# Entering RWKV time mixing by halves of tokens and features, with half of the split subtractions on POOL

## The reference

```python
h = rms_norm(x, g_mix[layer])
x = x + rwkv7_time_mix(h, ...)
...
h_prev = jnp.pad(h, ((0, 0), (1, 0), (0, 0)))[:, :-1]
hh = h_prev - h
xr = h + hh * mu[0]
xw = h + hh * mu[1]
xk = h + hh * mu[2]
xv = h + hh * mu[3]
xa = h + hh * mu[4]
xg = h + hh * mu[5]
r = xr @ w_r
w = -jax.nn.softplus(-(w0 + jnp.tanh(xw @ w1) @ w2)) - 0.5
k = xk @ w_k
v = xv @ w_v
a = jax.nn.sigmoid(a0 + (xa @ a1) @ a2)
g = jax.nn.sigmoid(xg @ g1) @ g2
```

## Time and profile before

| what | us |
|---|---|
| three runs: median (lowest to highest) | 1528.77 (1528.56 to 1530.85) |
| the profiled execution: its own time | 1527.23 |
| its span in the profile | 1525.4 |
| PE busy in the span | 1419.9 |
| DVE busy | 921.0 |
| ACT busy | 723.3 |
| POOL busy | 156.4 |

### The profile page before, as it was taken

How to read it: one execution, slowest core, us unless ns; L and a number is a source line. 1 busy time by engine, 2 the same in 40 slices (tenths; PEclk the granted TensorE clock), 3 DMA queues, 4 the chain that set the end, 5 groups by cost and what they waited for, 6 DMA issues and landing times.

```text
span 1525.4 us, 25988 instructions
## 1 busy us (share of the span) xinstructions
PE 1419.9 (93%) x10678; PEld 1214.7 (80%) x10678; DVE 921.0 (60%) x1250; ACT 723.3 (47%) x974; POOL 156.4 (10%) x132
## 2 busy tenths in 40 slices
PE   8998999998999999979988987999999968799998
PEld 8966988887988899867767765799997745589997
DVE  5565655566566645569868687465455655455563
ACT  5464545446545545445644342454445645254452
POOL 0162011100000111010120111000000232000000
PEclk9999999999999999989989999999999989799999
DMA  8733565555545655644442000556464531246562
GB/s 294 240 93 111 188 191 186 183 165 189 191 152 165 214 173 175 209 150 131 145 146 84 4 4 18 161 177 208 152 226 152 166 96 42 83 151 195 159 210 88
DMA packets 82262, 231.32 MB, mean 152 GB/s; under 512 B 11696, under 2 KB 17472, under 8 KB 82144
## 3 DMA queue, kind: packets, MB, share of 16 engines
q1 hardware_dynamic: 81584, 227.54, 46.6%
q0 software_dynamic: 560, 2.11, 0.4%
HBM read 228.56 MB, written 1.06 MB: 151 GB/s over the span
## 4 chain that ended last, share of the span: by engine, by line
PE 77%; DVE 8%; issue 5%; ACT 4%; POOL 3%; DMA 1%; DVEq 0%; ACTq 0%; POOLq 0%; SPq 0%
PE PS L410 48%; PE PS L413 26%; PE PS L425 4%; ACT SH L382 1%; POOL SM L539 1%; DVE XI L1264 1%; POOL AB L770 1%; DVE SL L385 1%; DVE SL L388 1%; DVE AB L744 1%; POOL QK L1895 0%; POOL SM L836 0%; ACT JK L542 0%; ACT AB L754 0%; DVE LG L1552 0%
## 5 line engine op out<-in xcount | busy, mean ns | idle before, releaser
L388 DVE SCALAR_TENSOR_TENSOR SL<-ST,SM,SH 128x1024 fp32r<-128x1024 f32 (+1 forms) x256 | 314.8, 1249 | 171.8 <-ACT SH L382 121.7
L382 ACT ACTIVATE SH<-ST,SM 128x1024 fp32r<-128x1024 f32 (+1 forms) x256 | 282.2, 1121 | 219.7 <-PE PS L413 133.1
L410 PE MATMUL PS<-XH,SH 128*128 128x256 f32 x1256 | 353.3, 281 | 2.6 <-DVE XL L1269 1.3
L413 PE MATMUL PS<-XH,SL 128*128 128x256 f32 x1256 | 353.4, 281 | 0.0
L410 PE MATMUL PS<-XL,SH 128*128 128x256 f32 x1256 | 352.4, 281 | 0.0
L385 DVE TENSOR_TENSOR SL<-ST,SH 128x1024 fp32r<-128x1024 f32 (+1 forms) x167 | 215.8, 1308 | 155.4 <-ACT SH L382 137.9
L410 PE MATMUL PS<-SH,XH 128*128 128x512 f32 x576 | 240.0, 417 | 26.6 <-DVE XL L1753 8.3
L382 ACT ACTIVATE SH<-ST 128x1024 fp32r<-128x1024 f32 (+1 forms) x167 | 172.1, 1047 | 177.6 <-PE PS L413 151.8
L410 PEld LDWEIGHTS PS<-XH,SH 128*128 128x128 f32 x1256 | 237.3, 189 | 4.2 <-ACT SH L382 3.0
L410 PEld LDWEIGHTS PS<-XL,SH 128*128 128x128 f32 x1256 | 235.1, 187 | 0.9
L413 PEld LDWEIGHTS PS<-XH,SL 128*128 128x128 f32 x1256 | 235.2, 187 | 0.2
(11 more groups left out here) (312 smaller groups left out, 1450.7 us busy)
## 6 DMA issues: line engine op xcount, KB each, us to landing
ST<-in_ffn_w_gu SPq DMA_DIRECT2D x80, 512.0 KB, 4.7
ST<-in_w_mlp_up SPq DMA_DIRECT2D x64, 512.0 KB, 4.8
ST<-in_w_mlp_down SPq DMA_DIRECT2D x64, 512.0 KB, 4.4
ST<-in_ffn_w_down SPq DMA_DIRECT2D x44, 512.0 KB, 4.3
ST<-in_w_attn_in SPq DMA_DIRECT2D x24, 512.0 KB, 5.2
ST<-in_w_conv_in SPq DMA_DIRECT2D x24, 512.0 KB, 4.5
ST<-in_w_ple_gate SPq DMA_DIRECT2D x16, 512.0 KB, 4.2
ST<-in_kv_w SPq DMA_DIRECT2D x16, 512.0 KB, 4.2
```

What stands on the lines that cost most here:

```text
L382: a = ac.do(lambda e: e.activation(h[p0:p1, 0:cols], t[p0:p1, 0:cols], ACT.Copy, scale=sc), ready, t_gt, pe_done.get(i - NSPLIT))
L388: b = ve.do(lambda e: e.scalar_tensor_tensor(l[p0:p1, 0:cols], t[p0:p1, 0:cols], sc, h[p0:p1, 0:cols].bitcast(F32), ALU.mult, ALU.subtract ...
L410: pe.go(lambda e: e.matmul(o, l, r, start=start, stop=stop, skip_group_check=skip))
L413: return pe.do(lambda e: e.matmul(o, l, r, start=start, stop=stop, skip_group_check=skip))
```

## The change

1. **Half of the weight subtractions on POOL.** From w_k on, every second unit's SL is written by POOL: w_k 1, 3, 5 and 7, the first half of g1, the unit with w2 and a2, four of w_r, four of w_v, and all eight of w_o. Before, DVE wrote them all.
2. **In `chain` of both `ple` calls** the gain's second half (XN, n = 1) goes to POOL, ahead of the power on that queue.
3. **Entering by halves of tokens.** `shift_chain(m)` writes XN = X by gain alone, and DG, the identity times the row factor. `shift_half(m)` makes the transposed, scaled half by 8 float32 matmuls of XN with DG. `shift_chain(0)` stands between the two chains of the first block; HT, HH and XI have other places in memory, so that they needn't wait for the second chain.
4. **Mixture 2 in quarters.** `mix_part` makes HH, XI, XH and XL for a half of features and a half of tokens. K's first four units run for tokens 0 to 127 (`k_half(0)`), then for the rest (`k_half(1)`), then the last four as before.
5. **Low parts of mixtures 1, 5, 4 and 0 on POOL** (mixture 3 was there before), those of mixture 2 for the features' second half too. The order of the first layers becomes w, g, a instead of w, a, g.
6. **The norm of KK by halves of tokens**: two powers of 16 columns on POOL instead of one of 32.

Idle products ahead of K are 4 and 2 instead of 8. PP, KK, GG and VN change places in memory.

```diff
+    r0 = len(units)
...
+    on_pool = set(range(r0 + 1, len(units), 2)) | set(range(len(units), len(units) + 8))
...
-            b = ve.do(lambda e: e.tensor_tensor(l[p0:p1, 0:cols], t[p0:p1, 0:cols], h[p0:p1, 0:cols].bitcast(F32), ALU.subtract),
-                      ready, a, pe_done.get(i - NSPLIT))
+            b = (po if i in on_pool and p0 == 0 else ve).do(lambda e: e.tensor_tensor(l[p0:p1, 0:cols], t[p0:p1, 0:cols], h[p0:p1, 0:cols].bitcast(F32), ALU.subtract),
+                                                ready, a, pe_done.get(i - NSPLIT))
...
-                vs.append(ve.do(lambda e, n=n: e.tensor_tensor(xs_[n], ee[n], g[:, n * 512:n * 512 + 512], ALU.mult), es[n], gt, xn_free[m]))
+                vs.append((po if n else ve).do(lambda e, n=n: e.tensor_tensor(xs_[n], ee[n], g[:, n * 512:n * 512 + 512], ALU.mult), es[n], gt, xn_free[m]))
...
-    ple_chain, _ = ple(1, before, 0)
-    for m in range(2):
-        ple_chain(m)
...
+    ple_chain, te1 = ple(1, before, 0)
+    HT = ar("HT", 8, [128, 8, S + 1])
+    HH = ar("HH", 11, [128, 8, S])
+    XI = ar("XI", 13, [128, 8, S])
+    t_mu = dma_once(small(256, 48), A["rw_muT"], c3)
...
+    def shift_chain(m):
+        ss = small(500 + m)
+        sq = squares(X[:, m, :], m, ss, xtok[m])
+        xg = ve.do(lambda e: e.tensor_tensor(XN[:, m, :], X[:, m, :], gm[0][:, :], ALU.mult), xtok[m], gm[1], xn_free[m])
+        st = rstd(ss, ss, D, 1e-6, sq)
+        dgs.append([ve.do(lambda e: e.tensor_scalar(DG[:, m, :], ID, ss, None, ALU.mult), st, sbt_free[0]), xg])
+        if m:
+            par_done(gm[2], xg)
+    def shift_half(m):
+        r = []
+        for n in range(2):
+            b = 4 + 2 * m + n
+            pe.wait(bfree[b], dgs[m])
+            for k in range(4):
+                c0 = n * 512 + k * 128
+                t = mm_t(bank(b, k * 128, k * 128 + 128), XN[:, m, c0:c0 + 128], DG[:, m, :], True, True)
+            cs, bs = slice(1 + m * 128, 129 + m * 128), slice(4 * n, 4 * n + 4)
+            ps = bank(b).rearrange("p (b t) -> p b t", b=4)
+            if n == 0:
+                r.append(ac.do(lambda e, ps=ps, bs=bs, cs=cs: e.activation(HT[:, bs, cs], ps, ACT.Copy), t, hr_free[0]))
+            else:
+                r.append(ve.do(lambda e, ps=ps, bs=bs, cs=cs: e.tensor_copy(HT[:, bs, cs], ps), t, hr_free[0]))
+            bfree[b] = r[n]
+        xn_free[m] = t
+        return r
...
+    z0 = ve.do(lambda e: e.memset(HT[:, :, 0:1], 0.0), hr_free[0], hx_free, te1)
+    ple_chain(0)
+    shift_chain(0)
+    ple_chain(1)
...
+    keep_busy(4, 0)
+    th = [shift_half(0)]
+    shift_chain(1)
...
-    th = norm_t(param(), 0, 0, to_ht)
-    t_hh = [ve.do(lambda e, bs=bs: e.tensor_tensor(HH[:, bs, :], HT[:, bs, 0:S], HT[:, bs, 1:S + 1], ALU.subtract), th, z0, xend)
-            for bs in (slice(0, 4), slice(4, 8))]
...
-    m2 = mix(2, 0)
-    keep_busy(8, 4)
-    wait_banks([0, 1, 2, 3])
-    pe.wait(m2[0], m2[2])
-    kind_a(XM[0], range(2), (0, 1, 2, 3), last=False)
-    m1 = mix(1, 1)
-    kind_a(XM[0], range(2, 4), (0, 1, 2, 3), first=False, last=False)
...
+    def mix_part(i, xs_i, g, m, eng):
+        xh, xl = XM[xs_i]
+        bs, cs, c1 = slice(4 * g, 4 * g + 4), slice(m * 128, m * 128 + 128), slice(1 + m * 128, 129 + m * 128)
+        a = ve.do(lambda e: e.tensor_tensor(HH[:, bs, cs], HT[:, bs, cs], HT[:, bs, c1], ALU.subtract), th[m][g], z0, hr_free[0])
+        t_hh[g] = a
+        for j in range(4 * g, 4 * g + 4):
+            t = ve.do(lambda e, j=j: e.scalar_tensor_tensor(XI[:, j, cs], HH[:, j, cs], small(256 + 8 * i + j), HT[:, j, c1],
+                                                            ALU.mult, ALU.add), a, t_mu, xi_free[g])
+        a = ac.do(lambda e: e.activation(xh[:, bs, cs], XI[:, bs, cs], ACT.Copy), t, xfree[xs_i])
+        b = eng.do(lambda e: e.tensor_tensor(xl[:, bs, cs], XI[:, bs, cs], xh[:, bs, cs].bitcast(F32), ALU.subtract), a, xfree[xs_i])
+        m2[g][m] = [a, b]
+    t_hh = [None, None]
+    m2 = [[None, None], [None, None]]
+    mix_part(2, 0, 0, 0, ve)
+    keep_busy(2, 0)
+    th.append(shift_half(1))
+    us = take_group(EDGE, EDGE - 1)
+    def k_half(m):
+        for j, (i, h, l) in enumerate(us):
+            pe.wait(split_tok[i], m2[0][m])
+            for n in range(2):
+                if j == 0:
+                    wait_banks([2 * m + n])
+                t = mm3(bank(2 * m + n), [x[:, j, m * 128:(m + 1) * 128] for x in XM[0]], [x[:, n * 512:(n + 1) * 512] for x in (h, l)], j == 0, False)
+            if m:
+                pe_done[i] = t
+    k_half(0)
+    mix_part(2, 0, 0, 1, ve)
+    for m in range(2):
+        mix_part(2, 0, 1, m, po)
+        xi_free[m] = [m2[m][0], m2[m][1]]
+    xi_free[0], xi_free[1] = m2[0], m2[1]
+    k_half(1)
     pe.wait(m2)
     kind_a(XM[0], range(4, 5), (0, 1, 2, 3), first=False, last=False)
-    m4 = mix(4, 2)
-    tk = kind_a(XM[0], range(5, 8), (0, 1, 2, 3), first=False)
+    m1 = mix(1, 1, po)
+    kind_a(XM[0], range(5, 7), (0, 1, 2, 3), first=False, last=False)
+    m5 = mix(5, 2, po)
+    tk = kind_a(XM[0], range(7, 8), (0, 1, 2, 3), first=False)
     xfree[0] = tk[1]
-    m5 = mix(5, 0)
-
-    i, h, l = take()
+    m4 = mix(4, 0, po)
+    iw, hw, lw_ = take(2)
     wait_banks([4, 5])
     pe.wait(m1, xend)
     for k in range(8):
-        t1 = mm3(bank(4, 0, 256), [x[:, k * 128:k * 128 + 128] for x in (h, l)], [x[:, k, :] for x in XM[1]], k == 0, k == 7)
+        t1 = mm3(bank(4, 0, 256), [x[:, k * 128:k * 128 + 128] for x in (hw, lw_)], [x[:, k, :] for x in XM[1]], k == 0, k == 7)
     xfree[1] = t1
+    ek = evac_a(KN, (0, 1, 2, 3), tk, xend)
+    m0 = mix(0, 1, po)
+    pe.wait(m5)
...
-    c = ve.do(lambda e: e.tensor_reduce(NS, hd(TT), AX.X, ALU.add), b)
-    c = ve.do(lambda e: e.tensor_scalar(NS, NS, 1e-24, None, ALU.max), c)
-    c = po.do(lambda e: e.tensor_tensor(NS, NS, MHW, ALU.pow), c)
+    cns = []
+    for m in range(2):
+        ns = NS[:, 16 * m:16 * m + 16]
+        c = ve.do(lambda e, m=m, ns=ns: e.tensor_reduce(ns, TT[:, m, :].rearrange("p (h d) -> p h d", d=64), AX.X, ALU.add), b[m])
+        c = ve.do(lambda e, ns=ns: e.tensor_scalar(ns, ns, 1e-24, None, ALU.max), c)
+        cns.append(po.do(lambda e, ns=ns: e.tensor_tensor(ns, ns, MHW[:, 0:16], ALU.pow), c))
```

55 lines of the change are left out of this document (23 added, 32 removed).

## The result

The changed kernel takes 1555.65 us (median of four runs, 1553.62 to 1556.74), the kernel before 1528.66 (four runs, 1527.73 to 1530.85). The ratio is 1.0173, with a 95% interval of 1.0155 to 1.0191: slower by 24 to 29 us. The prediction said 1548.5, with a range of 1531 to 1559. The profiled execution of the changed kernel took 1554.95, its span 1552.8.

What follows compares the result with a forecast made beforehand. PE was busy 93% of the span, with DVE nearly as full from K to the second layers. Terms 13.4 + 6 + 0.5 = 19.9 on the profiled 1527.2 gave 1547.1, plus 1.5 for the median, say 1548.5 us; range 1531 to 1559.

Steps and rivals of the forecast that it cites:

- Rival B: POOL and DVE overlap after all, POOL alone bounds the mixtures: second layers -2.1, in all -6.3, 1522.5 us; chance 0.15.
- C: Exclusion at the mixtures, but late in V DVE's products go ahead of w_o: +13.9, 1542.5 us; chance 0.25.
- D: Exclusion in part, POOL holding the memory for half its time: second layers +1.8, late V 0, 1531 us; chance 0.1.
- The entry: Way into RWKV: K begins near 688, 6.4 us earlier; its fifth unit waits for DVE until 702.7, gaining 2.9.
- The mixtures: From K to the second layers: PE waits for mixture 4's low part, second layers at 745.3 instead of 731.86, +13.4 us.
- The shared sum of 38.0 us: Between K and the second layers: mutually exclusive DVE and POOL time ahead of mixture 4 from 701.6, ready at 739.6.
- the third forecast wait: Before the second layers: PE waits some 4 us for POOL's XL ahead of a, after waits ahead of w and g.
- To R: Second layers to R: SGR's sums wait behind units 14 and 16, +1 at most, offset by KK's earlier norm; 0 taken.
- Late in V: From V's third unit to AGR: products and POOL's subtractions take 26.9 instead of 20.3 us; +6, between 0 and +9.
- After the scan: w_o's last three units move to POOL: scan steps grow or PE starts earlier, between -2.8 and +3.9 us, 0 taken.
- The first chain: The first block's other ple call: its chain(0), on which PE waits, grows by 0.5 us.
- two inputs: A large two-input POOL instruction and a DVE instruction with two SBUF inputs don't overlap at all, whichever came first.

Runs made afterwards that it cites:

- e7: The changed kernel with POOL's low parts of the units and mixtures 1, 5, 4, 0 and 3 made by a one-input copy instead of a subtraction; 1529.1 us.
- e8: The changed kernel with the addition of HT left out of DVE's XI in mixtures 1, 5, 4, 0 and 3, so one input; 1551.1 us.
- e5: e1 with all of XN on DVE and three moves in DVE's order (entry, mixture 1, mixture 0); 1527.5 us, ratio 0.9984 to the kernel before.
- e1: The changed kernel with all low parts but mixture 3's back on DVE, entry by halves and new order kept; 1534.2 us.

## Why the prediction was right, and where it was off

The direction, the cause and the range held. Rival B (the engines overlap) would have shown XI at 0.48 and POOL's XL at 2.41. C (V's products go first) fell with KK, TT and AGR, each of which waited for a POOL subtraction late in V, and D (POOL holds for half its time) with the second layers at +15.6, where it had +1.8. The sign that the prediction gave for C, a wait of 2 for AGR, would have misled: 3.3 lies nearer to it than to the 8 of the forecast. By its own steps:

- **The entry, -6.4 at K and -2.9 at the fifth unit:** measured -6.6 and -3.1. Right; of its terms, the second half's transposing products took 2.86 instead of 3.7.
- **The mixtures, +13.4 at the second layers:** measured +15.6. On the clock of before, mixture 4's last XL ends at 738.2 (739.6 predicted), w starts at 719.9 (719.4) and the first layers end at 742.2 (742.4). The shared sum of 38.0 us was right within 1.5. That the first layers ended just where they were forecast is partly luck: mixture 4 was ready 1.4 earlier, and the third forecast wait, 4 us ahead of a, didn't come, since PE's slow stretch in g took its place. The mis-sized term is LL: 2.9 us from a's last product to the second layers, and 5.3 measured. The prediction put one POOL subtraction in its way. On ACT, LF stood behind the high part of the second layers' unit and started 1.3 after a's end; on DVE, LL could have started at LH's end, 748.78, and stood 2.2 behind that unit's low part, which itself waited for POOL's XL:

```profile
744.87 4.97 POOL L1296 TENSOR_TENSOR XL<-XI,XH 128x1024 fp32r<-128x1024 f32 x2 [2.64 <-ACT XH L1293]
746.40 1.05 ACT L384 ACTIVATE SH<-ST 32x1024 fp32r<-32x1024 f32 x1
747.48 0.38 ACT L1379 ACTIVATE LF<-PS 64x256 f32<-64x256 f32 x1
747.56 3.35 DVE L387 TENSOR_TENSOR SL<-ST,SH 32x1024 fp32r<-32x1024 f32 x1 [2.28 <-ACT SH L384]
750.95 0.42 DVE L1383 TENSOR_TENSOR LL<-LF,LH 128x256 fp32r<-128x256 f32 x1
```

- **To R, 0:** +1.0. Within its bound.
- **Late in V, +6:** measured +4.0 from R's start to the transposes, but half of it lies elsewhere. In the stretch that the sum was made for, from DVE's small copy at V's third unit to the end of AGR, DVE took 22.4 us (817.87 to 840.27) instead of 20.4 (795.23 to 815.60): +2.0, where 26.9 and 20.3 were put down, and PE's wait for AGR was 3.3, not some 8. The sum took all six products into the turns; three of them had run or were running when POOL's first low part began at 824.3. It also counted five subtractions of DVE before, where the trace has four and an idle gap of 2.3. The other +2.0 were in no term: V's first product waited 4.3 instead of 3.3, now for RN's copy on DVE, and PE took 1.0 longer for the 32 short products ahead of V's third unit, at a granted clock of 0.58 instead of 0.69. The nearness of 4 to 6 is in part luck. DVE's copy at V's third unit, now and before:

```profile
817.87 0.19 DVE L1508 COPY SM<-PS 128x32 f32<-128x32 f32 x1 [7.09 <-PE PS L415]
795.23 0.19 DVE L1444 COPY SM<-PS 128x32 f32<-128x32 f32 x1 [6.70 <-PE PS L413]
```

- **After the scan, 0 (-2.8 to +3.9):** measured +3.3 in the shifts. DVE's own stretch, from RN's second product by SM to XL, tells it better: 13.9 to 14.0 us in all six profiled executions with w_o's subtractions on POOL, 10.0 in all seven with none there (9.4 in e7, where POOL copies): +3.9. This is the step that failed. The prediction took the middle because no row told which engine wins when both are ready. They take turns, so three POOL subtractions cost three products of RN 2.2 us each, 6.6, less the 3.4 that DVE no longer spends on w_o, plus 0.7 that it now idles ahead of XL, 3.9: the upper bound was the value.
- **The first chain, +0.5:** 0.5 by the chain's own length (4.83 and 5.33). To the convolution stage the changed kernel's trace has 0.8 more, of which the rest isn't told from the variation between executions.

The terms measured give 15.6 + 1.0 + 4.0 + 3.3 + 0.8 = 24.7, where 19.9 was predicted. The ratio's interval says 23.7 to 29.2. So what the medians show beyond the prediction is the step after the scan and LL for the most part, less what late V fell short. Single shifts carry an error of up to 3.6 us, so the terms are no finer than that, and whether the rest of some 2 us is the change's isn't settled: the profiled execution has its 3.3 ahead of 350 us, and there the program is the same.

**What the words "two inputs" had wrong.** The prediction named two inputs on both sides. The runs show: on POOL a subtraction or product over 512 to 2048 columns, and a copy with one input as well (e7); on DVE two inputs from SBUF, or the faster form with one (e8). Whether POOL's reading or its writing holds DVE no run separates. What reads PSUM isn't held up, nor is a reduction with one input: DVE's TENSOR_REDUCE of 2048 columns took its usual 2.27 us beside POOL's subtraction above, which itself ended 2.2 us after AGR. The Trainium skill, SBUF — State Buffer, section Who interferes with whom, states these cases in this form: two SBUF inputs on DVE against a GpSimd instruction that reads SBUF, and DVE's 2-port modes against any, a tensor_reduce never. The rows agree with the first and the last: XI at 2.56 us, TENSOR_REDUCE at its usual 2.27. The one-input form at 2.42 agrees with the second, if its faster pace is such a mode, which the rows don't name. The sum of the prediction needed only the first.

One kind of POOL instruction doesn't fit "reads SBUF", as that section has it, and "POOL's duration" doesn't price it: the power. In the kernel before it takes 6.37 us for 32 columns with both inputs in SBUF, and DVE's subtraction with two inputs from SBUF, issued in the middle of it, takes its usual 1.23:

```profile
765.90 6.37 POOL L1411 TENSOR_TENSOR SM<-SM 128x32 f32<-128x32 f32 x1 [9.95 <-DVE SM L1410]
768.68 1.23 DVE L385 TENSOR_TENSOR SL<-ST,SH 128x1024 fp32r<-128x1024 f32 x1 [1.71 <-ACT SH L382]
```

By the section's rule it would have been held; the rows decide. An instruction of few columns can be long on POOL and yet leave DVE alone; all that is shown held up above stood beside 512 columns or more.

**Where the entry's gain went.** It was real, 6.6 us at K, and worth half at the fifth unit (5.8 of 7.4 with DVE's queue in another order, e5), because DVE is as full there as PE. With all these low parts on DVE (e1) it was gone at the second layers. PE's waits there name the new order (mixture 4 last, LL behind mixture 0); the share of the halves' short instructions on DVE isn't shown by itself. Only with DVE's idle gaps filled (e5) did the stage come out even.

## What to carry to other kernels

Elementwise work over hundreds of columns, moved from DVE to POOL beside DVE's own SBUF work, isn't moved off DVE: for each instruction, add POOL's duration to DVE's and take off DVE's own. It pays only where POOL's duration is below DVE's, or where DVE at that place reads PSUM, reduces, or idles. Where POOL has to work beside DVE's critical chain, cut its work into short instructions, since each engine waits for one instruction of the other.

When two engines are both nearly full, bringing one of them an earlier start gives nothing; look for idle gaps in the fuller one's queue first. And where no row shows which of two engines is served first, a step between two bounds isn't known to its middle: give both bounds, or find a row that shows the order. Here the dear end came true after the scan, and less than a third of the forecast late in V.

## What the runs showed of the hardware

- DVE and POOL alternate one for one when both have work that excludes the other: XI of 0.48 us took 2.56 and 2.59 in turn with POOL's subtractions of 2.92 and 2.55; with pieces of half the size a product's wait fell from 2.2 to 1.1.
- The size of DVE's instruction doesn't decide if it waits: one of a single column took 0.89 instead of 0.16 beside POOL's 1.67. Nor does POOL's time alone decide: beside a power of 32 columns and 6.37 us, DVE's subtraction took its usual 1.23.
- POOL copies 1024 columns in 1.04 us and subtracts them in 2.4, 2.3 times as long.
- With the same instructions on all engines, fourteen executions reach the power at 350 us between 350.20 and 354.00; the two of the kernel before differ there by 3.6. From K to the second layers these two differ by 3.6 as well.
